# Query latents projected from x times the norm weight, with the factor per token applied on VectorE, and a table copy moved behind two cached-latent products

## The reference, cut to what matters

```python
def rms(x, g):
    return xf * lax.rsqrt(jnp.mean(xf * xf, axis=-1, keepdims=True) + RMS_EPS) * g

h = rms(x, lp['norm_mix'])
proj = h @ lp['w_in']                      # q_lat, kv_lat, k_rp, ... are columns of it
q = rms(q_lat, lp['mla_q_norm']) @ lp['mla_wq_b']
kv = concat(past_ckv, rms(kv_lat, ...)) @ lp['mla_wkv_b']
```

## Time and profile before

| | |
|---|---|
| Median of 3 runs | 933.67 us (933.37 to 934.33) |
| Profiled execution, its own time | 933.06 us |
| Its span (first to last instruction) | 931.3 us |
| Mean granted TensorE clock | 0.999 |
| PE busy | 922.5 us (99%) |
| DVE busy | 495.3 us (53%) |
| POOL busy | 444.4 us (48%) |
| ACT busy | 204.2 us (22%) |
| DMA | 113.02 MB, mean 121 GB/s |

### The profile page before, as it was taken

The page is one execution under the profiler, slowest core; times in us unless marked ns, Lnnn a source line. Parts: engine busy times, 40 slices in busy tenths (PEclk is TensorE's granted clock), DMA queues, the critical chain, the costliest instruction groups (busy, mean ns, idle before and its releaser), DMA issues.

```text
span 931.3 us, 14894 instructions
## 1 busy us (share of the span) xinstructions
PE 922.5 (99%) x5718; PEld 811.5 (87%) x5718; DVE 495.3 (53%) x1009; ACT 204.2 (22%) x445; POOL 444.4 (48%) x469
## 2 busy tenths in 40 slices
PE   8999999999999999999999999999999999999998
PEld 6777877777999999999977678777799999999998
DVE  5474656854565656512253565578357565563221
ACT  2224264531100000100031243562310000110001
POOL 6210380124966666676411205503168666666670
PEclk9999999999999999999999999999999999999999
DMA  9959412119544544443443773112555555534321
GB/s 279 231 132 69 141 47 91 50 15 253 137 136 137 137 137 139 133 146 125 123 128 108 61 147 95 46 48 50 124 149 140 142 144 144 148 123 135 126 95 41
DMA packets 159635, 113.02 MB, mean 121 GB/s; under 512 B 10246, under 2 KB 157356, under 8 KB 159436
## 3 DMA queue, kind: packets, MB, share of 16 engines
q1 hardware_dynamic: 154660, 104.50, 38.8%
q0 software_dynamic: 4272, 6.80, 7.1%
q10 hardware_dynamic: 632, 0.75, 0.3%
HBM read 108.46 MB, written 2.27 MB: 119 GB/s over the span
## 4 chain that ended last, share of the span: by engine, by line
PE 97%; DVE 1%; DMA 1%; ACT 0%; issue 0%; SPq 0%; ACTq 0%; DVEq 0%
PE ps L1128 52%; PE ps L776 20%; PE ps L1085 7%; PE ps L1146 2%; PE ps L885 1%; PE ps L857 1%; PE ps L982 1%; PE ps L922 1%; PE ps L1023 1%; PE ps L1032 1%; PE ps L804 1%; PE ps L824 1%; PE ps L965 1%; DMA arena<-in_x_sample 1%; PE ps L1043 1%; PE ps L1064 0%
## 5 line engine op out<-in xcount | busy, mean ns | idle before, releaser
L776 PE MATMUL ps<-hT,ring 128*128 128x320 f32 x672 | 187.8, 435 | 2.2 <-DVE hT L1597 1.7
L776 PEld LDWEIGHTS ps<-hT,ring 128*128 128x128 f32 x672 | 124.5, 190 | 54.8 <-DVE hT L1597 3.9
L601 POOL TENSOR_TENSOR work<-ring 128x512 f32<-128x512 f32 (+1 forms) x66 | 81.8, 1239 | 154.5 <-issue 113.3
L1128 PE MATMUL ps<-mixT,ring 128*128 128x160 f32 x672 | 105.0, 299 | 0.0
L1128 PE MATMUL ps<-hT,work 128*128 128x160 f32 x672 | 98.5, 299 | 0.0
L1128 PE MATMUL ps<-hT,ring 128*128 128x160 f32 x672 | 98.1, 299 | 0.0
L1128 PEld LDWEIGHTS ps<-mixT,ring 128*128 128x128 f32 x672 | 95.8, 190 | 0.0
L1128 PEld LDWEIGHTS ps<-hT,ring 128*128 128x128 f32 x672 | 93.7, 190 | 0.3
L1128 PEld LDWEIGHTS ps<-hT,work 128*128 128x128 f32 x672 | 93.7, 190 | 0.0
L603 POOL TENSOR_TENSOR work<-ring 128x512 f32<-128x512 f32 (+1 forms) x66 | 82.2, 1246 | 5.2
L602 POOL TENSOR_TENSOR ring<-ring 128x512 f32<-128x512 f32 (+1 forms) x66 | 82.2, 1246 | 5.2
(11 more groups left out here) (392 smaller groups left out, 1351.6 us busy)
## 6 DMA issues: line engine op xcount, KB each, us to landing
ring<-in_w_gu SPq DMA_DIRECT2D x88, 512.0 KB, 5.2
ring<-in_w_in SPq DMA_DIRECT2D x44, 512.0 KB, 7.1
ring<-in_w_down SPq DMA_DIRECT2D x32, 512.0 KB, 4.5
ring<-in_w_out SPq DMA_DIRECT2D x16, 512.0 KB, 4.5
ring<-in_w_down SPq DMA_DIRECT2D x16, 384.0 KB, 3.5
cst<-in_consts POOLq DMA_DIRECT2D x1, 1664.0 KB, 12.3
ring<-in_w_in SPq DMA_DIRECT2D x2, 640.0 KB, 5.5
arena<-r POOLq DMA_DIRECT2D x8, 160.0 KB, 17.0
```

The source lines that it names most:

```text
L601: step(tt(s3, a11, a21, ALU.subtract))
L776: ins = mm(bank(use, 0, T, m), w[:, k, c:c + m], hT[:, k, 0:T], start=(k == 0), stop=(k == KT - 1))
L1128: ins = mm(bank(use, at * HT, HT), left, right(k), start=(opens and k == 0 and at == 0), stop=(closes and k == n - 1), skip_group_check=True)
```

## The change

In both layers the query latents are projected from `xgm` = xT * norm_mix (it takes the place of `mixT`, which is free at that time), and no longer from hT. In layer 0 DVE makes the eight tiles of xgm with tensor_scalar, straight after the copy of the norm weights and ahead of `normalise`; the weights' transposition is moved into the sum of squares, ahead of its fifth product. In layer 1 ACT makes each tile with one activation (Copy, the weight as scale) behind its square. PE waits per tile for `mix_gained`, in ql1 too; the wait for all normalised tiles stands now ahead of kvr. In layer 1 the first half of ql0 stands ahead of `norm_sum`, the second half behind it. In layer 0 two of the four cached-latent products stand ahead of PE's wait for the second `cols_ready`.

DVE's `query_latents(p)` multiplies the bank by rstd into `qls` (new), then the bank by the norm weight and rstd into `qlT` (scalar_tensor_tensor in place of tensor_scalar). ACT squares `qls` in place, after the first of the two, where it squared the bank. The clears and the sum of squares stand in `latent_sum`, in layer 0 behind the key copies. Some semaphores are merged into others (kvr_ms with gif_abs, kvr_rstd with gif_ln, q_squared with q_rstd); each wait is for the same instruction as before.

```diff
--- before.py
+++ after.py
@@ -332,6 +332,7 @@
         a3 = work[:, MSLOTS * 3 * 512:MSLOTS * 3 * 512 + (FT // 2) * 3 * HT].rearrange("p (k s n) -> p k s n", s=3, n=HT)
         xg = work[:, MSLOTS * 3 * 512:MSLOTS * 3 * 512 + KT * T].rearrange("p (k n) -> p k n", k=KT)
         h3 = mixT[:, :, :].rearrange("p k n -> p (k n)")[:, 0:3 * 4 * HT].rearrange("p (s k n) -> p s k n", s=3, k=4)
+        xgm = mixT
         dhf = dh[:, :, :].rearrange("p a n -> p (a n)")
         ysq = dhf[:, 0:NT * G].rearrange("p (t h e) -> p t h e", t=NT, h=H)
 
@@ -745,8 +746,13 @@
 
             turn_x(range(0, KT // 2))
             turn_x(range(KT // 2, KT))
+            pe.wait_ge(sem("x_turned"), 1)
             claim(pe, "ms1", 0)
             for n, k in enumerate((0, 2, 4, 5, 6, 7)):
+                if n == 4:
+                    pe.wait_ge(sem("gain_rows"), 16)
+                    nc.tensor.transpose(ps[:, 0, 0:NGAIN], rows[0:NGAIN, :], ident[0:NGAIN, 0:NGAIN]).then_inc(
+                        sem("rows_turned"), 1)
                 if n < 2:
                     pe.wait_ge(sem("sq_pairs"), n + 1)
                 else:
@@ -764,16 +770,16 @@
                     ins = mm(bank(use, 0, T), C("ones"), hT[:, k, 0:T], start=(n == 0), stop=(k == KT - 1))
                 fill(ins, use)
 
-            def feature(use, l, name, c, m, wait_h=False, ks=range(KT)):
+            def feature(use, l, name, c, m, right=hT, ks=range(KT)):
 
                 if ks[0] == 0:
                     claim(pe, use, l)
                     wait_chunk(pe, name, l)
                 w = chunk(name, l, 256)
                 for k in ks:
-                    if wait_h:
-                        need(pe, "normed", l, KT, k + 1)
-                    ins = mm(bank(use, 0, T, m), w[:, k, c:c + m], hT[:, k, 0:T], start=(k == 0), stop=(k == KT - 1))
+                    if right is not hT:
+                        pe.wait_ge(sem("mix_gained"), l * KT + k + 1)
+                    ins = mm(bank(use, 0, T, m), w[:, k, c:c + m], right[:, k, 0:T], start=(k == 0), stop=(k == KT - 1))
                 if ks[-1] == KT - 1:
                     fill(ins, use)
 
@@ -844,12 +850,6 @@
 
             for l in range(DEPTH):
 
-                if l == 0:
-                    pe.wait_ge(sem("gain_rows"), 16)
-                    pe.wait_ge(sem("x_turned"), 1)
-                    nc.tensor.transpose(ps[:, 0, 0:NGAIN], rows[0:NGAIN, :], ident[0:NGAIN, 0:NGAIN]).then_inc(
-                        sem("rows_turned"), 1)
-
                 def latents_out(tiles):
                     for i in tiles:
                         claim(pe, f"kv{i}", l)
@@ -859,24 +859,27 @@
                 if l > 0:
                     need(pe, "past_T", l, 1)
                     latents_out(PAST_TILES[0:2])
+                    feature("ql0", l, "ql", 0, P, xgm, range(0, 4))
                     norm_sum("ms1", l)
+                    feature("ql0", l, "ql", 0, P, xgm, range(4, KT))
                     latents_out(PAST_TILES[2:])
-                if l > 0:
                     pe.wait_ge(sem("recleared"), 6 * l)
-
-                feature("ql0", l, "ql", 0, P, wait_h=True)
-                feature("ql1", l, "ql", P, P, ks=range(0, 6))
+                else:
+                    feature("ql0", l, "ql", 0, P, xgm)
+                feature("ql1", l, "ql", P, P, xgm, range(0, 6))
                 if l == 0:
                     past_latents(0)
-                feature("ql1", l, "ql", P, P, ks=range(6, KT))
+                feature("ql1", l, "ql", P, P, xgm, range(6, KT))
                 if l == 0:
                     pe.wait_ge(sem("rows_loaded"), 16 * len(ROWLOADS))
                     pe.wait_ge(sem("x_turned"), KT)
                     nc.tensor.transpose(ps[:, 7, 0:NROWS], rows[:, :], ident[0:NROWS, 0:NROWS]).then_inc(
                         sem("rows_turned"), 1)
+                    need(pe, "past_T", l, 1)
+                    latents_out(PAST_TILES[0:2])
                     pe.wait_ge(sem("cols_ready"), 2)
-                    need(pe, "past_T", l, 1)
-                    latents_out(PAST_TILES)
+                    latents_out(PAST_TILES[2:])
+                need(pe, "normed", l, KT)
                 claim(pe, "kvr", l)
                 wait_chunk(pe, "kvr", l)
                 w = chunk("kvr", l, 168)
@@ -1311,6 +1314,9 @@
                     else:
                         need(act, "x_new", l, 2 * KT, k + 1)
                     step(A(hT[:, k, 0:T], xT[:, k, :], ACT.Square), "squared")
+                    if which == 0 and l > 0:
+                        A(xgm[:, k, :], xT[:, k, :], ACT.Copy, scale=col("norm_mix", l * KT + k)).then_inc(sem("mix_gained"), 1)
+                        act.wait_ge(sem("mix_gained"), l * KT + k + 1)
                     if which == 1:
                         step(A(xg[:, k, :], xT[:, k, :], ACT.Copy, scale=col("norm_ffn", l * KT + k)), "x_gained")
 
@@ -1341,8 +1347,8 @@
                         step(A(ksq[:, :, :], kv[:, :, 0:HD], ACT.Square), "k_squared")
 
                 def latent_squares(p):
-                    wait_filled(act, f"ql{p}", l)
-                    step(A(qls[:, p, 0:T], bank(f"ql{p}", 0, T), ACT.Square), "qlat_sq")
+                    need(act, "qlat_raw", l, 2, p + 1)
+                    step(A(qls[:, p, 0:T], qls[:, p, 0:T], ACT.Square), "qlat_sq")
 
                 need(act, "arena_b", l, 1)
                 if l > 0:
...
@@ -1673,6 +1679,10 @@
                     dve.wait_ge(sem("pre_filled"), KT)
                     dve.wait_ge(sem("rows_turned"), 1)
                     step(v.tensor_copy(cols[:, 0:NGAIN], ps[:, 0, 0:NGAIN]), "cols_ready")
+                    for k in range(KT):
+                        v.tensor_scalar(xgm[:, k, :], xT[:, k, :], col("norm_mix", k), None, ALU.mult).then_inc(
+                            sem("mix_gained"), 1)
+                        dve.wait_ge(sem("mix_gained"), k + 1)
                 now_made(dve, "arena_b")
                 normalise(l, "norm_mix")
 
@@ -1685,13 +1695,16 @@
                         step(v.tensor_reduce(small[:, 72 + 4 * i:76 + 4 * i], ksq[:, :, :], AX.X, ALU.add), "k_ms")
 
                 def query_latents(p):
-                    need(dve, "qlat_sq", l, 2, p + 1)
-                    step(v.tensor_scalar(qlT[:, p, 0:T], bank(f"ql{p}", 0, T), col("q_norm", 2 * l + p), None, ALU.mult))
+                    wait_filled(dve, f"ql{p}", l)
+                    step(v.tensor_tensor(qls[:, p, 0:T], bank(f"ql{p}", 0, T), rstd[:, :], ALU.mult), "qlat_raw")
+                    step(v.scalar_tensor_tensor(out=qlT[:, p, 0:T], in0=bank(f"ql{p}", 0, T), scalar=col("q_norm", 2 * l + p),
+                                                in1=rstd[:, :], op0=ALU.mult, op1=ALU.mult))
                     now_read(dve, f"ql{p}")
-                    if p == 0:
-                        return
+
+                def latent_sum():
                     step(v.memset(qlT[:, :, T:TP], 0.0), "qlat")
                     step(v.memset(qls[:, 0, T:TP], 0.0))
+                    need(dve, "qlat_sq", l, 2)
                     step(v.tensor_tensor(qls[:, 0, 0:T], qls[:, 0, 0:T], qls[:, 1, 0:T], ALU.add), "qlat")
 
                 if l > 0:
@@ -1705,6 +1718,7 @@
                 query_latents(1)
                 if l == 0:
                     key_copies(PAST_TILES, 0)
+                latent_sum()
                 wait_filled(dve, "kvr", l)
                 kvr = bank("kvr", 0, 504).rearrange("p (t n) -> p t n", t=NT)
                 step(v.tensor_copy(mift[:, :, :], kvr[:, :, 160:168]), "mif_copied")
...
```

More of the change, by code:

```diff
@@ L1357, in _ @@
                     key_stats(PAST_TILES, 0)
-                need(act, "kvr_ms", l, 1)
+                need(act, "kvr_gif_args", l, 2, 1)
                 step(A(small[:, 0:NT], small[:, 8:8 + NT], ACT.Ln, scale=1.0 / KVR, bias=eps_c[:, :]))
                 step(A(small[:, 3:3 + NT], small[:, 11:11 + NT], ACT.Ln, scale=1.0 / ROPE, bias=eps_c[:, :]))
-                step(A(small[:, 0:6], small[:, 0:6], ACT.Exp, scale=-0.5), "kvr_rstd")
+                step(A(small[:, 0:6], small[:, 0:6], ACT.Exp, scale=-0.5), "kvr_gif_done")
                 if l == 0:
                     act.wait_ge(sem("cols_ready"), 2)
-                need(act, "gif_abs", l, 1)
+                need(act, "kvr_gif_args", l, 2, 2)
                 step(A(lfr[:, :], lfr[:, :], ACT.Exp, scale=-1.0))
-                step(A(lfr[:, :], lfr[:, :], ACT.Ln, bias=one_c[0:H, :]), "gif_ln")
+                step(A(lfr[:, :], lfr[:, :], ACT.Ln, bias=one_c[0:H, :]), "kvr_gif_done")
                 if l == 0:
@@ L1395, in _ @@
                 step(A(qsq[:, :, :, :].rearrange("p t h e -> p (t h e)"),
-                       qtm[:, :, :, :].rearrange("p t h e -> p (t h e)"), ACT.Square), "q_squared")
+                       qtm[:, :, :, :].rearrange("p t h e -> p (t h e)"), ACT.Square), "q_stats")
                 need(act, "q_ms", l, 1)
@@ L1399, in _ @@
```

(14 more changed lines are left out.)

## The result

The changed kernel takes 934.87 us in the median of 20 runs (933.78 to 936.89), the kernel before 933.38 in 20 runs beside it (933.04 to 935.17): a ratio of 1.0015, 95% interval 1.0009 to 1.0021. That is 1.5 us slower, clear of noise and inside the predicted 932.4 to 937.1; the forecast, +0.34 us, had under a quarter of the difference. The profiled execution of the changed kernel has a span of 933.6 us, 2.3 more than before.

The account below looks back on a forecast made before the run. PE, busy for 99% of the span, was taken as the bound, with only its gaps to win. Layer 0's -0.16 and layer 1's +0.50 us gave +0.34 on 933.67, so 934.0 us; range 932.4 to 937.1.

Parts of the forecast that it names:

- The start of layer 0: Layer 0, ql0's first product: starts at 13.44 instead of 15.32, 1.88 us earlier, and finds each tile ready.
- The new wait in layer 0: Layer 0, before the cached-latent products: PE waits 2.2 us for ACT's latents copy and starts at 25.25, where it was 25.41.
- the gain of 2.4 us ahead of it: Layer 0, ahead of the cached-latent products: some 2.4 us won, of which 0.16 us stays.
- Layer 1: Layer 1, kvr: the factor comes 1.81 us later, PE waits 1.5 us for bank 0, kvr starts 0.50 us later.
- the sum: Whole kernel: layer 0's -0.16 and layer 1's +0.50 add up to +0.34 us; chance of this forecast 0.53.
- the slower rival: Layer 0: DVE's new tiles hold up POOL's DMAs, wkvb lands 2.4 to 3.1 us later; 936.4 to 937.1 us; chance 0.30.
- The faster rival: Layer 0's cached-latent products and layer 1's kvr: the two new waits don't bind; 930.3 us; chance 0.10.

Follow-up runs that it names:

- e1: The changed kernel with ACT's copy of the cached latents in layer 0 moved ahead of its square of ql0: 931.65 us, ratio 0.9973.
- e2: The changed kernel with DVE's reading of ql0 moved ahead of the copies of keys 3 and 5 in layer 1: 933.94 us, ratio 0.9996.
- e3: The changed kernel with ACT's latents copy ahead of its square in layer 0 and DVE's ql0 ahead of the keys in layer 1: 930.36 us, ratio 0.9959.
- e6: The changed kernel with ACT's latents copy first in layer 0 and the sum of squares ahead of all of ql0 in layer 1: 930.87 us, ratio 0.9967.
- e4: The changed kernel with three discarded products on PE before its wait for the cached latents in layer 0: 933.88 us, ratio 0.9998.
- e5: The kernel before with six unused ACT squares ahead of its latents copy in layer 0, so PE idles there: 935.26 us, ratio 1.0021.
- e3b: e3 run once more, unchanged, in another set: 931.10 us, ratio 0.9962.

## Why the prediction was right or wrong

**The start of layer 0** was right in kind: ql0's first product at 13.77 (13.44 forecast), right behind the sum and unbroken, so the first tile wasn't what it waited for. The sum was: its last product starts 0.47 us later than before. Around the transposition two steps of 0.27 became 0.52 and 0.37, so it cost 0.36 us where 0.13 was forecast, and 0.16 came earlier, ahead of the second pair of squares. DVE's eight tiles took 4.00 us instead of 3.4, hidden.

```profile
12.43 0.23 PE L754 MATMUL ps<-cst,work 16*128 16x16 f32 x1
12.59 1.34 PE L760 MATMUL ps<-hT,cst 128*128 128x320 f32 x4
13.01 4.00 DVE L1683 TENSOR_SCALAR mixT<-xT,cols 128x320 f32<-128x320 f32 x8
```

**The new wait in layer 0** was right to 0.02 us: the products at 25.23, 25.25 forecast, released by ACT's latents copy; the gain of 2.4 us ahead of it had shrunk to 0.18 (0.16 forecast). e1 shows that this one order held it. That the number is so close is partly luck: PE was forecast to turn the latents at 21.35, held by wkvb's DMA, and did so at 21.31, but held by nothing. The DMA had landed at 21.04, and PE's own way was 0.33 late from ql0's first product on. Two misses cancelled.

**Layer 1** was right: the sum 1.8 us late, PE waiting 1.29 us (1.5 forecast) at kvr, +0.45 us (+0.50). e2, e3 and e6 each remove it.

**What failed is the sum**, "-0.16 + 0.50 = +0.34". It has two terms too few. The first is the clock: I priced the wait in layer 0 at its length and said nothing of the products behind it, though the working had just made it 2.2 us of idle PE. It is worth 1.7 us in the profiled execution. In the runs it divides the changed kernel in two halves, ten runs of 933.78 to 934.36 at full clock and ten of 935.37 to 936.89 at 0.998; their medians are 934.0 and 935.5, and the one over all lies between, at 934.87. e4 removes it with the wait's end unmoved, e5 makes it without the change. The second is 0.27 us at L1042, which starts 2.93 us after L1035's first product (599.35 and 602.28), where it was 2.66 (L1032 and L1039 in the kernel before, 597.30 and 599.96). The rows of the changed kernel:

```profile
599.35 1.04 PE L1035 MATMUL ps<-cst,arena 128*128 128x128 f32 x8
602.28 0.41 PE L1042 MATMUL ps<-arena 128*128 128x64 f32 x2 [0.16 <-ACT arena L1469]
```

With both, the profiled execution adds up: -0.18 + 1.70 + 0.45 + 0.27 = 2.24, spans 2.3 apart. Without the clock it is +0.54, and the full-clock runs at 934.0 are 0.6 above the median of before. So of the 1.5 us measured the two waits that the forecast was made of explain 0.27, under a fifth. That the measured time lies within the range is luck in part: its upper bound was the price of the slower rival, and no bound took in the clock.

**The slower rival** (0.30) gave the right sign by a mechanism that didn't happen. POOL's issues beside the tiles took 0.92, 0.74 and 0.69 (0.58 before for the last), and wkvb's DMA landed 7.3 us after its issue, 7.4 before. DVE's tiles of the changed kernel (durations in ns, min/median/max):

```profile
L1683 DVE TENSOR_SCALAR mixT<-xT,cols x8: 385/454/567, 13.0 to 16.4; 128x320 f32<-128x320 f32 x8
```

They are what was slower, with 454 ns in the middle and 567 at most, where one of 323 columns elsewhere takes 389. The three slowest (556 to 567 ns) are the last three, from 15.25 on, beside POOL's next four issues, which took 2.41 us in all (2.39 before). That POOL's issues are the cause fits, but no run took them away:

```profile
14.45 2.41 POOL L637 DMA_DIRECT2D work<-in_state_mlstm_C  x4
```

The starving of the queue that "SBUF — State Buffer" (§ SBUF: two separate sides) of the Trainium skill describes did not show here.

**The faster rival** (0.10) was rightly small for the kernel as changed; its size was right: 930.3 forecast for both waits gone, 930.36 measured in e3 (931.10 in e3b, another set), and for layer 0's alone 931.8 against 931.65 in e1.

## What to carry to other kernels

When an edit lets an engine run ahead, follow each in-order queue that its next operand passes: here one copy on ACT, needed by PE, stood behind a square that the edit had made wait for a chain over DVE and PE itself. Price an idle time of PE not by its length alone: ask what the clock is behind it, and look at the spread of the runs as well as at their median, since it may fall in half of them only. Moving that one copy ahead (e1) was worth 3.2 us, more than the edit around it, and three cheap discarded products in the idle time (e4) were worth 1.0 us, both compared across two sets of runs.

## What the hardware showed that was not expected

- After 2.1 us of idle PE the granted clock was 0.68 and 0.55 over the next 4.3 us, and eight instructions took 5.40 instead of 3.70 us; in another kernel (e2) the same wait was followed by 3.70. After 1.3 us of idle time it stayed at 1.00 in this trace.
- A tensor_scalar on DVE beside POOL's DMA issues took up to 567 ns for 385 at best, and wkvb's DMA, issued beside them, landed 7.3 us behind its issue, 7.4 before.
- In nine profiled executions ACT started a copy some 0.3 us late with nothing shown to wait for, a DMA of kind "instruction" of 8 KB started 0.6 to 1.2 us behind that start, and with eight instructions fewer on ACT 120 us earlier the delay was gone.
